# Normalised h made from the transposed chunks instead of turned token rows, indexer keys projected before the norm, query halves doubled by DMA

## Chip, cores and metric

One Trainium2 chip, one core. The number is the device time in microseconds (us) of one execution of the whole kernel.

## What is computed

One layer of a hybrid encoder block on x of 512 tokens by 1024 channels, in fp32. What matters here is the first part, the norm, the input projection and the indexer of the sparse branch:

```python
h = rmsnorm(x, g_pre_mix[l])                  # x * rsqrt(mean(x*x) + eps) * g, one factor per token
proj = h @ w_in[l]
(qa, ka, va, qi, ki, wi, qb, kb, vb, gate_a, gate_b) = split_columns(proj)
# indexer: 8 heads of 64, one shared key of 64, one weight per head and token
dots  = relu(einsum('bqhd,bsd->bqhs', qi, ki) * IDX_DIM ** -0.5)
score = einsum('bqhs,bqh->bqs', dots, wi * N_IDX_HEADS ** -0.5)
top_val, top_idx = lax.top_k(where(admissible, score, -inf), 128)
```

After it come sparse attention over the chosen keys, a stick-breaking attention, gates, an output projection and a SwiGLU MLP of width 2816. The change leaves those alone.

## The kernel before

Every engine (TensorE, ScalarE or ACT, VectorE or DVE, GpSimd or POOL, SyncE or SP) runs a list of instructions written out by hand, and the lists meet at semaphores. Each fp32 product is made of three fp32r products: an operand `a` is split into `a_hi` (rounded by ACT) and `a_lo = a - a_hi` (made by DVE or POOL), and TensorE adds hi*hi, hi*lo and lo*hi. So nothing can be multiplied before ACT has rounded it and DVE or POOL has made the rest.

The start of the kernel goes as follows.

- `first` holds, for each of 8 chunks of 128 channels, the transposed x (512 tokens) beside the indexer-query columns of `w_in` (512 columns). `chunk_rows` (L320) loads a chunk as one 512 KB transfer into a ring `xf` of four. ACT rounds both halves (`round_x` L864 with the gain g folded in, `round_wq` L868), DVE makes `xg_lo` (`rest_x` L1364), POOL makes `wq_lo` (`rest_wq` L1211), and TensorE runs three passes of four 512-column matmuls per chunk (`first_pass` L551, loop L556 to L574) into banks 0 to 3. These queries are not normalised: the token factor r is positive, so it can be moved past the relu into the head weights `w_tok` (L1404).
- The normalised h, for all other projections, is made from token rows: four blocks `x_in` of 128 tokens are loaded, ACT squares them (`square_x` L857), DVE and ACT make r = 1/sqrt(var) per block, DVE scales the rows by r and by the gain (`norm_x` L1368; the gain row was spread over partitions by TensorE, L564 to L568), TensorE turns each block with eight transposes (`turn_x` L537), ACT rounds it (`round_turned` L852) and DVE makes the rest (`rest_turned` L1356). The turns lie between the chunks 2 to 5 of the query projection.
- Then 24 matmuls make the indexer key and head weights from h (L579 to L584, called the kw stage below), and `heads_b_steps` (L603) starts the first two tiles of the other projections, interleaved with `indexer_scores(h)` (L586) for the eight heads. A head's scores are hi and lo query parts against the key; `qi_twice` holds each head's rounded query twice, on partitions 0 to 63 and 64 to 127, and ACT writes both copies out of PSUM (L907 to L910), 16 half-height instructions.
- ACT applies the relu (L923, L924), DVE adds up the weighted scores (L1413 to L1424), 24 instructions, then takes the top 128 in rounds of eight. `indexer_scores(h)` waits for the relu of head h-2.
- The value projection V follows (L633 to L640). Its weight tiles 0 and 1 are rounded by ACT before the queries (L899, L900), tiles 2 and 3 after them and before the first relu (L912, L913). POOL makes the rest of tile 2 only after `idx_summed` reached 8, the end of the score sums (L1251 to L1262).

SP issues the loads in one queue, in order. A weight pair d goes into half of the buffer `raw` and waits for `w_lo_done` of pair d-2 and for the landing of pair d-1 (`pair`, L340 to L350). V's tiles 2 and 3 are the pair of the second turn of the loop at L370.

```python
        for t in range(PAIRS):
            ...
            for h in range(2):
                r, o = slice(HD * h, HD * h + HD), slice(HD - HD * h, P - HD * h)
                run(qi_twice[r, 2 * t + h, :], ps[r, t, :], ACT.Copy).then_inc(qi_hi_done, 1)
                run(qi_twice[o, 2 * t + h, :], ps[r, t, :], ACT.Copy).then_inc(qi_hi_done, 1)
```

Of the kernel before, what the change touches and what calls it, by code (L numbers as in the profile page):

```python
# [28 lines left out]
P = 128  # L29
# [22 lines left out]
WARM = 14  # L52
# [71 lines left out]
def build(nc, first, gain_cols, first_kw, x, w_in, w_branch_sparse, w_branch_sb, w_out, w_gate_up, w_down,  # L124
# [75 lines left out]
    xf = sb("xf", [RING, 1024])  # L200
# [61 lines left out]
    small_in, kw_in, g_cols_in, g_row_in = sems("small_in", "kw_in", "g_cols_in", "g_row_in")  # L262
    first_in = sems(*(f"first_in{c}" for c in range(KC)))
# [55 lines left out]
    def _(sp):  # L319
        def chunk_rows(c):  # L320
# [49 lines left out]
        loop(T_V, KC // 2, v_rows)  # L370
# [75 lines left out]
    def _(pe):  # L446
# [80 lines left out]
        def first_part(k, tile, u, t0, t1):  # L527
# [3 lines left out]
            pe.wait_ge(h_lo_done, k * TB + t1)  # L531
# [46 lines left out]
        pe.wait_ge(h_lo_done, TB)  # L578
        for c in range(KC):  # L579
            acc = ps[0:KW, 6, :]  # L580
            mm(acc, kw_hi[:, c, :], h_hi[:, c, :], start=c == 0, stop=False)
            mm(acc, kw_hi[:, c, :], h_lo[:, c, :], start=False, stop=False)
            ins = mm(acc, kw_lo[:, c, :], h_hi[:, c, :], start=False, stop=c == KC - 1)
        ins.then_inc(kw_done, 1)  # L584

        def indexer_scores(h):  # L586
# [3 lines left out]
            if h == 0:  # L590
                pe.wait_ge(qi_rest_done, 1)
                pe.wait_ge(ki_halves_done, 3)
                pe.wait_ge(w_tok_done, 1)
            if h == 1:
                pe.wait_ge(qi_rest_done, PAIRS)
            for b in (3, 2, 1):
# [163 lines left out]
        for i in range(4):  # L760
            first_part(1, T_UP, i, 0, 2)
# [927 lines left out]
```

## Time and profile before

| | |
|---|---|
| median of three runs | 788.36 us (787.41 to 788.89) |
| the profiled execution, its own time | 788.59 us |
| its span in the trace | 786.8 us |
| TensorE matmul busy | 777.3 us, 99% of the span |
| VectorE, ScalarE, GpSimd busy | 380.5, 357.3, 413.4 us |
| granted TensorE clock, mean | 0.999 |

The span is the time from the first to the last record of the trace; 1.8 us of the execution lie around it. A timeline row gives start and duration in us, the engine, the source line, the operation with output and input names, and in brackets how long the engine had been idle before it and what ended that. Durations of neighbouring matmuls overlap, since they are pipelined; the distance between two starts is what a matmul costs TensorE. A row "x4" merges four in a row.

### The profile page before, as it was taken

To read this page: it belongs to the slowest core of one execution; us is meant where nothing else is said; L and a number is where in the kernel's file an instruction comes from. 1 tells how busy PE (TensorE), PEld (TensorE's weight loads), DVE (VectorE), ACT (ScalarE), POOL (GpSimd) and SP (SyncE) were. 2 spreads that over 40 slices of the span, in tenths; PEclk is the share of its full clock that TensorE was granted. 3 is DMA by queue.
4 is the path that set the end of the run, shared out by engine and by line. 5 is a ranking of instruction groups with operands and counts; after the bars stand their busy time and mean duration, and the time that the engine had idled before them with its cause. 6 is when DMAs were issued, how large, how long until landed. Compare 5 with 4: busy or idle time off the path is not lost.

```text
span 786.8 us, 10511 instructions
## 1 busy us (share of the span) xinstructions
PE 777.3 (99%) x3700; PEld 649.8 (83%) x3700; DVE 380.5 (48%) x540; ACT 357.3 (45%) x572; POOL 413.4 (53%) x250
## 2 busy tenths in 40 slices
PE   9999999999999999999999999999999999999997
PEld 6788888888888888888888988888888888888885
DVE  5689959999566665299137000000000020544564
ACT  6774177767686766542265222222212222232242
POOL 5666255866768687243560334444344443444462
PEclk9999999999999999999999999999999999999999
DMA  9321443113222422212491123333223332233312
GB/s 345 107 100 47 141 121 107 55 54 95 72 62 68 114 61 81 81 54 107 137 318 54 55 66 94 107 107 106 74 86 107 107 107 81 80 107 107 107 54 107
DMA packets 100011, 79.40 MB, mean 101 GB/s; under 512 B 2817, under 2 KB 90889, under 8 KB 99978
## 3 DMA queue, kind: packets, MB, share of 16 engines
q1 hardware_dynamic: 99978, 78.97, 31.9%
q8 instruction: 20, 0.33, 0.2%
q14 instruction: 13, 0.11, 0.0%
HBM read 76.85 MB, written 3.68 MB: 102 GB/s over the span
## 4 chain that ended last, share of the span: by engine, by line
PE 92%; DVE 5%; ACT 1%; issue 0%; DMA 0%; DVEq 0%; SPq 0%
PE ps L478 24%; PE ps L457 19%; PE ps L458 19%; PE ps L459 19%; PE ps L553 2%; PE ps L702 2%; PE ps L691 2%; PE ps L674 1%; PE ps L676 1%; DVE keep_buf L1471 1%; PE ps L498 1%; DVE e_buf L1479 1%; DVE h_lo L1360 1%; PE ps L600 1%; PE ps L599 1%; DVE k_both L1431 0%
## 5 line engine op out<-in xcount | busy, mean ns | idle before, releaser
L1171 POOL TENSOR_TENSOR w_lo<-raw,w_hi 128x1024 fp32r<-128x1024 f32 x74 | 177.1, 2394 | 248.3 <-ACT w_hi L813 219.9
L457 PE MATMUL ps<-h_hi,w_hi 128*128 128x512 f32 (+1 forms) x608 | 235.7, 388 | 0.3 <-DVE h_lo L1360 0.3
L459 PE MATMUL ps<-h_hi,w_lo 128*128 128x512 f32 (+1 forms) x608 | 233.8, 385 | 0.0
L458 PE MATMUL ps<-h_lo,w_hi 128*128 128x512 f32 (+1 forms) x608 | 233.7, 384 | 0.0
L813 ACT ACTIVATE w_hi<-raw 128x1024 fp32r<-128x1024 f32 (+1 forms) x70 | 74.1, 1060 | 271.2 <-PE ps L459 192.1
L459 PEld LDWEIGHTS ps<-h_hi,w_lo 128*128 128x128 f32 x608 | 114.3, 188 | 22.5
L457 PEld LDWEIGHTS ps<-h_hi,w_hi 128*128 128x128 f32 x608 | 114.4, 188 | 21.7 <-issue 0.7
L458 PEld LDWEIGHTS ps<-h_lo,w_hi 128*128 128x128 f32 x608 | 114.4, 188 | 21.0
L1623 DVE TENSOR_TENSOR act<-silu,ps 128x512 f32 (+1 forms) x22 | 15.1, 688 | 211.3 <-PE ps L459 211.3
L1271 POOL TENSOR_TENSOR w_lo<-raw,w_hi 128x1024 fp32r<-128x1024 f32 x30 | 77.7, 2593 | 30.5 <-ACT w_hi L948 30.1
L1628 DVE TENSOR_TENSOR d_lo<-act,d_hi 128x512 fp32r<-128x512 f32 x18 | 43.0, 2395 | 51.7 <-ACT d_hi L1111 51.7
L478 PE MATMUL ps<-w_hi,d_hi 128*128 128x512 f32 x144 | 44.4, 389 | 0.0
L478 PE MATMUL ps<-w_lo,d_hi 128*128 128x512 f32 x144 | 44.4, 389 | 0.0
L478 PE MATMUL ps<-w_hi,d_lo 128*128 128x512 f32 x144 | 44.3, 389 | 0.0
L1180 POOL TENSOR_TENSOR q_lo<-proj,q_twice 64x512 fp32r<-64x512 f32 x16 | 26.8, 1675 | 29.6 <-ACT q_twice L827 28.5
L1508 DVE TENSOR_TENSOR a_lo<-ps,a_hi 128x1280 fp32r<-128x1280 f32 x16 | 23.8, 1489 | 23.7 <-ACT a_hi L995 23.6
L995 ACT ACTIVATE a_hi<-ps 128x1280 fp32r<-128x1280 f32 x16 | 19.9, 1246 | 28.3 <-PE ps L691 28.3
L948 ACT ACTIVATE w_hi<-raw 128x1024 fp32r<-128x1024 f32 x30 | 31.9, 1063 | 0.2
L478 PEld LDWEIGHTS ps<-w_lo,d_hi 128*128 128x128 f32 x144 | 27.0, 188 | 5.7
L478 PEld LDWEIGHTS ps<-w_hi,d_lo 128*128 128x128 f32 x144 | 27.0, 188 | 5.6
L478 PEld LDWEIGHTS ps<-w_hi,d_hi 128*128 128x128 f32 x144 | 27.0, 188 | 5.6
L1471 DVE TENSOR_TENSOR_SCAN keep_buf<-keep_buf,ends 128x1280 f32<-128x1280 f32 x8 | 26.1, 3268 | 10.6 <-ACT keep_buf L976 10.5
(212 smaller groups left out, 1342.9 us busy)
## 6 DMA issues: line engine op xcount, KB each, us to landing
raw<-in_w_gate_up SPq DMA_DIRECT2D x44, 512.0 KB, 4.5
raw<-in_w_in SPq DMA_DIRECT2D x40, 512.0 KB, 4.2
raw<-in_w_down SPq DMA_DIRECT2D x22, 512.0 KB, 3.9
xf<-in_first SPq DMA_DIRECT2D x8, 512.0 KB, 6.1
raw<-in_w_out SPq DMA_DIRECT2D x8, 512.0 KB, 4.1
x_in<-in_x SPq DMA_DIRECT2D x4, 512.0 KB, 7.7
raw<-in_w_branch_sb SPq DMA_DIRECT2D x8, 256.0 KB, 3.0
raw<-in_w_branch_sparse SPq DMA_DIRECT2D x8, 256.0 KB, 2.9
```

Source lines behind the costliest of these rows:

```text
L457: mm(acc, whi_c, a_hi_, start=first, stop=False)
L458: mm(acc, whi_c, a_lo_, start=False, stop=False)
L459: return mm(acc, wlo_c, a_hi_, start=False, stop=last)
L478: ins = mm(bank(2 * t + n), a[:, t * P:(t + 1) * P], w[:, slot, n * 512:(n + 1) * 512], start=first and p == 0, stop=last and p == 2)
L813: run(w_hi[:, at(u), :], raw[:, at((d % 2) * 2 + u), :], ACT.Copy).then_inc(w_hi_done, 1)
L948: run(hi[:, slot, :], raw[:, (T_FILL + k) % 4, :], ACT.Copy).then_inc(w_hi_done, 1)
L1171: nc.gpsimd.tensor_tensor(w_lo[:, at(u), :], raw[:, at((d % 2) * 2 + u), :], w_hi[:, at(u), :], sub).then_inc(w_lo_done, 1)
L1180: nc.gpsimd.tensor_tensor(q_lo[r, h, :], proj[r, 2 * g, :], q_twice[r, h, :], sub).then_inc(q_lo_done, 1)
L1271: nc.gpsimd.tensor_tensor(lo[:, slot, :], raw[:, (T_FILL + k) % 4, :], hi[:, slot, :], sub).then_inc(w_lo_done, 1)
L1471: nc.vector.tensor_tensor_scan(keep_buf[:, ::-1], keep_buf[:, ::-1], ends[:, ::-1], 1.0, ALU.mult, ALU.max).then_inc(scan_done, 1)
L1508: tt(a_lo[:, :], z(1, 0, TRI), a_hi[:, :], sub).then_inc(a_lo_done, 1)
L1628: tt(d_lo[:, at(u), :], act[:, at(j * 2 + u), :], d_hi[:, at(u), :], sub).then_inc(d_lo_done, 1)
```

## The change

- The rows are no longer normalised or turned. When all four blocks are squared, r is made for all tokens at once; DVE lays it as four diagonal matrices (`diag`), and one fp32 matmul of `ones` against them (inside chunk 5) puts r of every token on all partitions in bank 7. Then DVE makes h for a chunk as x_t * g * r into banks 4 and 5 in turn (`make_h`), ACT rounds it (`round_h`) and DVE makes the rest (`rest_h`): a ring of three steps per chunk, eight chunks.
- The gain row and its matmuls are gone. All of transposed x stays in `x_t`; a chunk is loaded as two transfers of 256 KB.
- The kw stage works on xg, the x before the norm; DVE then multiplies the key by r (`ki`), and the head weights take r twice. `kw_lo` moves from DVE to POOL.
- ACT rounds each pair of query heads once, full height, into `qi_hi` (`round_qi`); SP then copies it into `qi_twice` with four transfers of 64 partitions for each pair, 16 in all, from SBUF to SBUF, each of 128 KB. They stand in SP's queue behind V's tiles 0 and 1 and ahead of V's tiles 2 and 3. `qi_lo` has full height, and the zeros are in `ki_hi` now.
- TensorE warms up with nine fp32 matmuls on a tile of zeros, released by DVE, instead of 14 transposes of `ident`, released by POOL. The head weights are turned by transposes instead of fp32 matmuls. `gain_cols` is loaded from ACT's queue.
- POOL makes the bias rows in two parts, the second after V's tiles 0 and 1.

```diff
@@ SP
+        def chunk_in(c):
+            sp.dma_start(x_t[:, c, :], first[c, :, 0:S]).then_inc(x_t_in[c], 16)
             if c >= RING:
-                sp.wait_ge(xg_lo_done, c - RING + 1)
                 sp.wait_ge(wq_lo_done, c - RING + 1)
-            sp.dma_start(xf[:, c % RING, :], first[c, :, :]).then_inc(first_in[c], 16)
+            sp.dma_start(wq_raw[:, c % RING, :], first[c, :, S:2 * S]).then_inc(wq_in[c], 16)
...
-        loop(T_V, KC // 2, v_rows)
+        pair(T_V // 2, 0, v_rows)
+        for t in range(PAIRS):
+            sp.wait_ge(qi_hi_done, t + 1)
+            for h in range(2):
+                for o in range(2):
+                    sp.dma_start(qi_twice[HD * o:HD * o + HD, 2 * t + h, :].bitcast(F32),
+                                 qi_hi[HD * h:HD * h + HD, t, :].bitcast(F32)).then_inc(qi_twice_in[t], 16)
+        with sp.Fori(1, KC // 2) as j:
+            pair(j + T_V // 2, j, v_rows)
@@ TensorE
-        pe.wait_ge(const, 2)
+        pe.wait_ge(warm_done, 1)
         for _ in range(WARM):
-            nc.tensor.transpose(bank(4)[:, 0:P], ident[:, :], ident[:, :])
+            mm(bank(4)[:, 0:P], warm[:, :], warm[:, :], start=True, stop=True)
...
             first_pass(wq_hi, xg_hi, c, c == 0, False)
+            if c == 5:
+                pe.wait_ge(small_kept, 1)
+                pe.wait_ge(diag_done, 1)
+                mm(bank(7), ones[:, :], diag[:, :, :].rearrange("p t n -> p (t n)"), start=True, stop=True).then_inc(r_spread, 1)
...
-            if c == 0:
-                pe.wait_ge(g_row_in, 16)
-                for n in range(2):
-                    ins = mm(bank(6 + n), one_row[:, :], g_in[:, n * 512:(n + 1) * 512], start=True, stop=True)
-                ins.then_inc(gain_spread, 1)
-            if 2 <= c < 2 + TB:
-                turn_x(c - 2)
-            if c == 2 + TB:
+            if c == 1:
+                pe.wait_ge(const, 2)
+                nc.tensor.transpose(bank(5, P), ident[:, :], ident[:, :]).then_inc(ident_turned, 1)
+            if c == 3:
                 pe.wait_ge(small_in, 16)
...
+            if h % 2 == 0:
+                pe.wait_ge(qi_twice_in[h // 2], 64)
@@ ScalarE
-        for c in range(1, KC):
+        for c in range(1, TB + 1):
             round_x(c)
             round_wq(c)
-            if 2 <= c < 2 + TB:
-                root(0, c - 2)
-            if c <= TB:
-                square_x(c - 1)
-            if c >= TB:
-                round_turned(0, c - TB)
+            square_x(c - 1)
+        sc.wait_ge(var_done[0], 1)
+        run(std[:, 0:TB], var[:, 0:TB], ACT.Sqrt).then_inc(root_done[0], 1)
+        for c in range(TB + 1, KC):
+            round_x(c)
+            round_wq(c)
+            round_h(c - TB - 1)
         sc.wait_ge(kw_in, 16)
         run(kw_hi[:, :, :], kw_raw[:, :, :], ACT.Copy).then_inc(kw_hi_done, 1)
         split(T_QKB // 2, 0)
+        round_h(3)
+        sc.wait_ge(kw_lo_done, 1)
         split(T_QKB // 2, 1)
+        round_h(4)
+        round_qi(0)
...
@@ VectorE
+        def make_h(c):
+            if c >= 2:
+                ve.wait_ge(xh_lo_done, c - 1)
+            stt(bank(4 + c % 2), x_t[:, c, :], g_cols[:, c:c + 1], bank(7), ALU.mult, ALU.mult).then_inc(xh_made, 1)
...
+        for c in range(TB):
             rest_x(c)
...
+        rest_x(TB + 1)
+        ve.wait_ge(r_spread, 1)
+        make_h(0)
+        rest_x(TB + 2)
+        make_h(1)
+        rest_x(TB + 3)
+        for c in range(KC):
+            rest_h(c)
+            if c + 2 < KC:
+                make_h(c + 2)
+            if c == KC - 3:
+                rest_qi(0)
+        ve.wait_ge(kw_done, 1)
+        ve.wait_ge(r_kept, 1)
+        ki = ps[0:HD, 6, :]
+        tt(ki, ki, r_row[0:HD, :], ALU.mult).then_inc(ki_scaled, 1)
```

How the order moves on two queues. First SP, behind the loads of the start: before, from the load of the kw weights on (`ISA` and branch rows are the loop over V's tiles).

```order
L338 DMA kw_raw<-in_first_kw 128x576
L350 DMA raw<-in_w_in 128x8x128 x2
L358 UNCONDITIONAL_BRANCH
L358 ISA
L345 ISA [waits w_lo_done]
L350 ISA [waits raw_in]
L350 ISA
L350 DMA raw<-in_w_in 128x2x512
```

The same place now.

```order
L349 DMA kw_raw<-in_first_kw 128x576
L361 DMA raw<-in_w_in 128x8x128 x2
L361 DMA raw<-in_w_in 128x2x512 [waits raw_in]
L361 DMA raw<-in_w_in 128x2x512
L386 DMA qi_twice<-qi_hi 64x512 [waits qi_hi_done]
L386 DMA qi_twice<-qi_hi 64x512 x3
...
L386 DMA qi_twice<-qi_hi 64x512 [waits qi_hi_done]
L386 DMA qi_twice<-qi_hi 64x512 x3
L388 UNCONDITIONAL_BRANCH
```

Sixteen copies, in four groups that each wait for ACT, stand ahead of the loop that now loads V's tiles from tile 2 on.

Second ACT, from the last chunk's rounding to the first relu, before (the rows L909 and L910 are the 16 half-height query copies, eight of each, the other six pairs left out).

```order
L866 ACTIVATE xg_hi<-xf,g_cols 128x512
L869 ACTIVATE wq_hi<-xf 128x512
L855 ACTIVATE h_hi<-ps 128x8x128
L885 ACTIVATE kw_hi<-kw_raw 128x576
L813 ACTIVATE w_hi<-raw 128x1024 x2
L895 ACTIVATE wv_hi<-raw 128x1024 x2
L909 ACTIVATE qi_twice<-ps 64x512
L910 ACTIVATE qi_twice<-ps 64x512
...
L895 ACTIVATE wv_hi<-raw 128x1024 x2
L923 ACTIVATE relu_buf<-ps 128x896
```

The same place now (L880 and L884 round a chunk, L888 is `round_h`, L892 `round_qi`).

```order
L880 ACTIVATE xg_hi<-x_t,g_cols 128x512
L884 ACTIVATE wq_hi<-wq_raw 128x512
L888 ACTIVATE h_hi<-ps 128x512
L910 ACTIVATE kw_hi<-kw_raw 128x576
L827 ACTIVATE w_hi<-raw 128x1024
L888 ACTIVATE h_hi<-ps 128x512
L827 ACTIVATE w_hi<-raw 128x1024
...
L931 ACTIVATE wv_hi<-raw 128x1024 x2
L936 ACTIVATE wi_t<-ps 8x512
L931 ACTIVATE wv_hi<-raw 128x1024 x2
L948 ACTIVATE relu_buf<-ps 128x896
```

The rounding of h now stands, chunk by chunk, between the rounding of the inputs and ahead of the kw weights; V's tiles 2 and 3 still stand directly ahead of the first relu.

## Rows read from the trace of the kernel before

**Rows 1.** The page, part 1; and TensorE's waits from 60 us on.
```profile
PE 777.3 (99%) x3700; PEld 649.8 (83%) x3700; DVE 380.5 (48%) x540; ACT 357.3 (45%) x572; POOL 413.4 (53%) x250
...
PE ps L691 <- DVE att_out L1516: 0.6, 1, 0.6
```

**Rows 2.** Timeline of TensorE, 0 to 12 us (start, duration, engine, line, operation).
```profile
1.68 3.25 PE L549 MATMUL ps<-ident 128*128 128x128 f32 x14 [1.68 <-POOL ident L1166]
5.08 2.07 PE L553 MATMUL ps<-xg_hi,wq_hi 128*128 128x512 f32 x4 [0.16 <-ACT xg_hi L866]
...
9.20 1.98 PE L567 MATMUL ps<-g_in,one_row 1*128 1x512 f32 x4
11.10 1.19 PE L553 MATMUL ps<-xg_hi,wq_hi 128*128 128x512 f32 x4
```

**Rows 3.** Timeline of TensorE, 13 to 35 us.
```profile
13.94 1.07 PE L553 MATMUL ps<-xg_hi,wq_hi 128*128 128x512 f32 x4
...
16.67 1.03 PE L543 MATMUL ps<-ident,x_in 128*128 128x128 f32 x8
17.46 1.17 PE L553 MATMUL ps<-xg_hi,wq_hi 128*128 128x512 f32 x4
...
24.46 1.06 PE L543 MATMUL ps<-ident,x_in 128*128 128x128 f32 x8 [0.40 <-DVE h_lo L1360]
...
34.86 0.40 PE L581 MATMUL ps<-h_hi,kw_hi 128*72 128x512 f32 x1
```

**Rows 4.** Timeline of TensorE, 40 to 73 us.
```profile
40.43 0.40 PE L457 MATMUL ps<-h_hi,w_hi 128*128 128x512 f32 x1
...
43.26 1.05 PE L618 MATMUL ps<-ident,wi_t 8*128 8x8 f32 x8
...
47.09 0.39 PE L599 MATMUL ps<-ki_both,qi_twice 128*128 128x512 f32 x1
...
51.27 0.39 PE L599 MATMUL ps<-ki_both,qi_twice 128*128 128x512 f32 x1
...
72.06 0.70 PE L478 MATMUL ps<-wv_hi,h_hi 128*128 128x512 f32 x2
```

**Rows 5.** Timeline of ScalarE, 22 to 51 us.
```profile
22.28 0.71 ACT L866 ACTIVATE xg_hi<-xf,g_cols 128x512 fp32r<-128x512 f32 x1
...
46.05 2.00 ACT L895 ACTIVATE wv_hi<-raw 128x1024 fp32r<-128x1024 f32 x2
48.33 0.92 ACT L923 ACTIVATE relu_buf<-ps 128x896 f32<-128x896 f32 x1 [0.28 <-PE ps L600]
49.15 0.38 ACT L924 ACTIVATE relu_buf<-ps 128x256 f32<-128x256 f32 x1
...
50.47 0.63 ACT L818 ACTIVATE proj<-ps 128x512 f32<-128x512 f32 x1
```

**Rows 6.** Timeline of VectorE, 15 to 66 us.
```profile
15.41 0.75 DVE L1366 SCALAR_TENSOR_TENSOR xg_lo<-xf,g_cols,xg_hi 128x512 fp32r<-128x512 f32 x1 [0.29 <-ACT xg_hi L866]
...
37.53 1.39 DVE L1410 TENSOR_TENSOR qi_lo<-ps,qi_twice 64x512 fp32r<-64x512 f32 x2 [5.00 <-ACT qi_twice L910]
...
52.77 12.44 DVE L1423 SCALAR_TENSOR_TENSOR score<-relu_buf,w_tok,score 128x512 f32<-128x512 f32 x21
```

**Rows 7.** Timeline of GpSimd, 27 to 75 us.
```profile
27.80 1.28 POOL L1213 TENSOR_TENSOR wq_lo<-xf,wq_hi 128x512 fp32r<-128x512 f32 x1 [2.94 <-ACT wq_hi L869]
...
69.52 4.76 POOL L1235 TENSOR_TENSOR wv_lo<-raw,wv_hi 128x1024 fp32r<-128x1024 f32 x2
```

**Rows 8.** SP's queue, 2 to 4 and 36 to 45 us (start, duration, line).
```profile
3.34 0.42 SPq L325 DMA_DIRECT2D xf<-in_first  x1
...
37.20 1.08 SPq L350 DMA_DIRECT2D raw<-in_w_in  x2
```

**Rows 9.** Stretches of 0.5 us; last three numbers: granted clock, DMA share, GB/s.
```profile
39.00:39.50 0.50, 0.50 (x3) 0.28 (x2) 0.00 (x0) 0.47 (x2) 0.50 (x2) 1.00 0.91 352
...
41.50:42.00 0.50, 0.50 (x4) 0.42 (x3) 0.50 (x1) 0.48 (x2) 0.50 (x3) 1.00 0.07 21
```

More of the change, by code:

```diff
@@ L51 @@
 KW = HD + HEADS
-WARM = 14
+WARM = 9
 RING = 4
@@ L185, in build @@
     wi_t = sb("wi_t", S)
+    r_row = sb("r_row", S)
     top[0] = zone2 + 4 * 2 * TRI
@@ L577, in _ @@
         pe.wait_ge(kw_lo_done, 1)
-        pe.wait_ge(h_lo_done, TB)
         for c in range(KC):
             acc = ps[0:KW, 6, :]
-            mm(acc, kw_hi[:, c, :], h_hi[:, c, :], start=c == 0, stop=False)
-            mm(acc, kw_hi[:, c, :], h_lo[:, c, :], start=False, stop=False)
-            ins = mm(acc, kw_lo[:, c, :], h_hi[:, c, :], start=False, stop=c == KC - 1)
+            mm(acc, kw_hi[:, c, :], xg_hi[:, c, :], start=c == 0, stop=False)
+            mm(acc, kw_hi[:, c, :], xg_lo[:, c, :], start=False, stop=False)
+            ins = mm(acc, kw_lo[:, c, :], xg_hi[:, c, :], start=False, stop=c == KC - 1)
         ins.then_inc(kw_done, 1)
@@ L615, in _ @@
         pe.wait_ge(wi_t_done, 1)
-        pe.wait_ge(small_kept, 1)
+        pe.wait_ge(xh_made, KC)
+        pe.wait_ge(r_kept, 1)
         for t in range(TB):
-            ins = mm(ps[:, 7, t * HEADS:(t + 1) * HEADS], wi_t[HD:KW, t * P:(t + 1) * P],
-                     ident[HD:KW, HD:KW], start=True, stop=True)
+            ins = nc.tensor.transpose(ps[:, 7, t * HEADS:(t + 1) * HEADS], wi_t[HD:KW, t * P:(t + 1) * P],
+                                      ident[HD:KW, HD:KW])
         ins.then_inc(wi_done, 1)
@@ L864, in round_x, with round_h, round_qi @@
         def round_x(c):
-            sc.wait_ge(first_in[c], 16)
-            run(xg_hi[:, c, :], xf[:, c % RING, 0:S], ACT.Copy, scale=g_cols[:, c:c + 1]).then_inc(xg_hi_done, 1)
+            sc.wait_ge(x_t_in[c], 16)
+            run(xg_hi[:, c, :], x_t[:, c, :], ACT.Copy, scale=g_cols[:, c:c + 1]).then_inc(xg_hi_done, 1)
         def round_wq(c):
-            run(wq_hi[:, c, :], xf[:, c % RING, S:2 * S], ACT.Copy).then_inc(wq_hi_done, 1)
+            sc.wait_ge(wq_in[c], 16)
+            run(wq_hi[:, c, :], wq_raw[:, c % RING, :], ACT.Copy).then_inc(wq_hi_done, 1)
+        def round_h(c):
+            sc.wait_ge(xh_made, c + 1)
+            run(h_hi[:, c, :], bank(4 + c % 2), ACT.Copy).then_inc(xh_hi_done, 1)
+        def round_qi(t):
+            sc.wait_ge(chunk_done, KC)
+            run(qi_hi[:, t, :], bank(t), ACT.Copy).then_inc(qi_hi_done, 1)
+        sc.dma_start(g_cols[:, :], gain_cols).then_inc(g_cols_in, 16)
         nc.scalar.preload_act_table(ACT.Sqrt)
@@ L886, in _ @@
         split(T_QKB // 2, 0)
+        round_h(3)
+        sc.wait_ge(kw_lo_done, 1)
         split(T_QKB // 2, 1)
+        round_h(4)
+        round_qi(0)
+        round_h(5)
+        round_qi(1)
+        round_h(6)
+        round_qi(2)
+        round_h(7)
+        run(r_row[0:HD, :], ps[0:HD, 7, :], ACT.Copy).then_inc(r_kept, 1)
+        round_qi(3)
         def split_value(c):
@@ new lines, in _ @@
+        nc.vector.tensor_copy(ki_hi[0:HD, 0, :], ki).then_inc(ki_hi_done, 1)
+        nc.vector.tensor_copy(ki_both[0:HD, :], ki).then_inc(ki_halves_done, 1)
+        nc.vector.tensor_copy(ki_hi[HD:P, 1, :], ki).then_inc(ki_halves_done, 1)
+        ve.wait_ge(ki_hi_done, 1)
+        tt(ki_both[HD:P, :], ki, ki_hi[0:HD, 0, :], sub).then_inc(ki_halves_done, 1)
+        for t in range(1, PAIRS):
+            rest_qi(t)
+        ve.wait_ge(wi_done, 1)
+        for b in range(TB):
+            r = rstd[:, b:b + 1]
+            ins = ts(w_tok[:, b, :], ps[:, 7, b * HEADS:(b + 1) * HEADS], r, r, ALU.mult, ALU.mult)
@@ L1615, in _ @@
         second_norm(3)
[L1616 to L1617 removed]
+        rest_turned(2)
+        rest_turned(3)
         def up(j):
```

211 lines of the change are left out of this document (97 added, 114 removed).

## The prediction

> **What bounds the kernel.** I read the page first, then TensorE's waits, then the timelines of the first 75 us. TensorE is busy 99% of the span, and from 60 us on its largest wait is 0.6 us [rows 1]. So only two things can change the time: what TensorE issues less, and new idle time of TensorE. Both lie in the first 72 us; whatever the start of V's tile 2 (72.06, [rows 4]) gains or loses, the rest of the kernel carries along unchanged. A measurement here can tell 0.2%, 1.6 us, from no change. The sum is made against the profiled execution (788.59 us, 0.23 above the median).
>
> **To the start of chunk 1.** Before, 14 transposes took 3.25 us from 1.68 on, the first pass began at 5.08, and chunk 0 took until 9.20: 4.12 us for twelve matmuls that cost 2.73 at full speed (13.94 to 16.67, [rows 3]); the difference is the 1.2 GHz level [rows 2]. Two gain matmuls followed until 11.10, four records in 1.90 us, so an fp32 matmul is two records and costs 0.95 [rows 2]. Now the warm-up needs no `ident` and starts near 0.95. Nine fp32 matmuls are 18 records at 3.25/14 = 0.23: they end near 5.0, and the first pass starts about where it did. Chunk 0 costs between 2.73 (clock up before it) and 4.12; I take 3.4, the middle, since the activity starts 0.7 us earlier. The gain matmuls are gone. Chunk 1 starts at 8.4 instead of 11.10, bounds 7.8 and 9.1: **2.7 us earlier**. ACT can follow: it has no work between its chunks but the squares.
>
> **From chunk 1 to the kw stage.** Before it took 23.76 us (11.10 to 34.86): seven chunks of 2.73 are 19.1; four turns of 0.79 (16.67 to 17.46) are 3.2; a wait of 0.40; the small matmul and slower restarts are the other 1.1 [rows 2, 3]. The change removes turns, wait and restarts and adds one fp32 matmul (0.95) and one transpose (0.1): 20.5 without waits. But three waits are new.
> - DVE may not go past `small_turned` after chunk 3, and everything for r (rest of chunk 4, five small DVE and ACT steps, the diagonals) stands behind it: ACT, blocked on `var_done`, rounds chunk 5 some 2.9 us after chunk 3 ended. TensorE loses about 0.2.
> - r is spread inside chunk 5. Then `make_h(0)` (DVE, 0.76 like [rows 6], 15.41), `round_h(0)` (ACT, 0.63 like the 512-column copy from PSUM), `xg_hi` (0.71, [rows 5]) and `wq_hi` (0.6) run one behind the other, 2.8 us with their handshakes, while TensorE has 1.8 us left in chunk 5: 1.0 lost. In chunk 6 the same ring takes 2.8 and TensorE 2.75: nothing lost.
> - `kw_hi` stands behind `round_h(2)`, which waits for `make_h(2)` and `rest_h(0)`, and `kw_lo` is now POOL's: 576 columns at 1.28 for 512 [rows 7] are 1.44, before 0.75 on DVE. `kw_lo` ends at 31.7, TensorE is there at 30.0: 1.7 lost.
> Together 23.4, and the kw stage starts at 31.8 instead of 34.86: **3.1 earlier**. Most of what the turns gave goes into waits of the ring. If a DVE step with PSUM on both sides costs 1.0 instead of 0.76, another 0.7 to 1.5 is lost.
>
> **From the kw stage to the first scores.** kw costs 5.57 as before (34.86 to 40.43). The first four steps run against `h_lo`, which stays ahead. Then TensorE waits 0.5 for `wi_t` (ACT makes it behind four h chunks, four query copies, `r_row` and V's tiles 0 and 1), and four transposes save about 0.5 of eight fp32 records (1.05, [rows 4]). ACT's 16 half copies (0.6 each, 9.9 us with kw's) become four of 0.63. On DVE the key scaling adds 0.7, the query rests fall from eight of 0.70 [rows 6] to four; `w_tok` is ready at 43.9. First scores at 44.0 instead of 47.09: still **3.1 earlier**.
>
> **The SP queue and the first relu.** This step decides. ACT's first relu waits for V's tiles 2 and 3 being rounded (2.00 us, [rows 5]), and they for their load. Before, the load was issued at 37.20 and had landed at 41.55, 1 MB in 2.6 us [rows 8, 9], 4.5 us before ACT wanted it (46.05). Now 16 copies of 128 KB stand ahead of it. The first pair is rounded at 33.85; issuing costs 0.42 each [rows 8], data flow begins 1.7 us after an issue (37.20, and full flow by 39.0). The trace has no transfer from SBUF to SBUF and none of 64 partitions, so I bound a copy from the loads, 1.28 us for 512 KB over 128 partitions, 4 KB in each:
> - by bytes, a quarter: 0.32, hidden below the issue of 0.42;
> - by bytes in a partition, half: 0.64.
> I take 0.64, because a copy touches half the partitions at both its ends, so half the lanes idle twice. Then 16 copies end at 35.6 + 10.2 = 45.8, the load at 48.4 to 48.6, the roundings at 50.5, and the first relu starts at 50.5 instead of 48.33. The scores of head 2 wait for its end (1.2 later, [rows 5]): they start at 51.7 instead of 51.27 [rows 4], and TensorE, which could have started at 48.1, idles 3.6. DVE's sums (12.44 for seven heads, [rows 6]) follow in the same rhythm; the first one, slower before beside POOL, is no longer the limit. V's tile 2 still waits for POOL's 6.7 us behind the sums, and both arrive at 72.5. All 3.1 us are given back and 0.4 more: 788.6 + 0.4 = 789.0, or 788.9 against the median. **Forecast: no change.**
>
> The Trainium skill ("SBUF — State Buffer", Door 1: The DMA port swizzle) says that partitions 0 to 63 reach only 8 of 16 ports and measured 196 GB/s for them against 328 for all 128, at 1 MiB. At 196 GB/s a copy would take 0.67, an estimate from that page, and the sum would be 0.5 us more; by bytes alone it would be the first rival's time. No run here shows such a transfer yet.
>
> **Other edits.** Splitting a chunk into two loads adds eight issues of 0.42 in SP's queue, hidden: the queue is ahead of the data until chunk 4, and TensorE needs chunk 7 only at 27. Loading the gains from ACT brings them earlier, below the warm-up. POOL's bias rows end at 52 instead of 46 and are wanted by SP only at 76. Memsets moved in POOL lie in its idle time.
>
> **Rivals.**
> - *A: the copies go by bytes (0.32) or at least as fast as they are issued.* Then the load lands near 45.0, the first relu starts at 47.0, TensorE waits 0.2 or not at all and keeps 3.1 us: 785.5. For it: every load seen reaches 400 GB/s, and nothing is read from HBM. Against it: nothing in the trace fills only half the partitions. Anything between 0.42 and 0.64 gives 785.5 to 789.
> - *B: the copies cost more than 0.72 each.* A round trip per copy that isn't hidden would do it. Each 0.1 more delays the load, the first relu and V by 1.6 us; from 0.72 on the kernel is slower by over 0.2%; at 0.8 it is 788.6 + 0.4 + 2.6 = 791.6.
> - *C: TensorE's idle time of 3.6 us before head 2 drops its clock to 1.2 GHz.* No wait in this trace is that long. The price is that of chunk 0, 4.12 - 2.73 = 1.4, or more: 790.4.
>
> **How the numbers follow.** Forecast 0.50 (0.06 of it below 786.8, 0.38 within 0.2%, 0.06 above 789.9: an earlier or later rise of the clock moves it by 0.6, a dearer h ring by up to 0.7). A 0.33, of which 0.31 is faster. B 0.11 and C 0.06 are slower. Sums: faster 0.37, same 0.40, slower 0.23. The forecast's own range is 787.9 to 790.2. For 8 in 10 the range takes in A down to 784.9 and the lower part of B up to 791.2.
>
> **What would show it.** Right: chunk 1 at about 8.4, kw at about 31.8, the transfer records of the copies running back to back for some 10 us from 35.6, the loads of tiles 2 and 3 landing after 48, a wait of 3 to 4 us of TensorE at head 2's scores released by ACT's relu, and V's tile 2 near 72.5. Wrong: the copies done by 43, or that wait missing (A); the wait over 5 us (B); 512-column matmuls 0.43 apart after it (C); kw later than 33, which would put the error into the h ring.

## Result and profile after

The changed kernel takes **792.67 us** (median; 792.07 to 793.47) against 788.36 in the same session (787.41 to 789.88): ratio 1.0055, 95% interval 1.004 to 1.007. It is 4.3 us slower. The forecast was 788.9 with no change as the likeliest verdict, and 784.9 to 791.2 as its range; the time lies outside of it.

The page's first part answers to [rows 1]:

```profile
span 790.8 us, 10447 instructions
...
PE 775.8 (98%) x3667; PEld 648.0 (82%) x3667; DVE 374.1 (47%) x540; ACT 350.4 (44%) x562; POOL 412.2 (52%) x251
```

So do TensorE's waits (us in total, times, longest):

```profile
PE ps L610 <- ACT relu_buf L949: 4.1, 1, 4.1
PE ps L589 <- POOL kw_lo L1254: 1.3, 1, 1.3
PE ps L558 <- DVE warm L1397: 1.1, 1, 1.1
PE ps L562 <- ACT wq_hi L884: 0.9, 1, 0.9
PE ps L542 <- DVE y_buf L1388: 0.6, 1, 0.6
PE ps L610 <- DVE w_tok L1462: 0.5, 1, 0.5
```

TensorE is busy 1.5 us less than before (775.8 for 777.3), and yet the span is 4.0 longer: one wait of 4.1 us, before the scores of head 2, stands out. TensorE's timeline shows where the 3.1 us that the prediction gave to the first scores went (it answers to [rows 2, 3, 4]):

```profile
1.07 4.21 PE L558 MATMUL ps<-warm 128*128 128x128 f32 x18 [1.07 <-DVE warm L1397]
4.93 2.05 PE L562 MATMUL ps<-xg_hi,wq_hi 128*128 128x512 f32 x4
6.78 1.20 PE L562 MATMUL ps<-xg_lo,wq_hi 128*128 128x512 f32 x4
7.82 1.07 PE L562 MATMUL ps<-xg_hi,wq_lo 128*128 128x512 f32 x4
...
25.43 0.93 PE L562 MATMUL ps<-xg_hi,wq_hi 128*128 128x512 f32 x3 [0.86 <-ACT wq_hi L884]
...
32.48 0.42 PE L589 MATMUL ps<-xg_hi,kw_hi 128*72 128x512 f32 x1 [1.27 <-POOL kw_lo L1254]
...
44.80 0.47 PE L610 MATMUL ps<-ki_both,qi_twice 128*128 128x512 f32 x1 [0.48 <-DVE w_tok L1462]
...
53.34 0.80 PE L610 MATMUL ps<-ki_both,qi_twice 128*128 128x512 f32 x1 [4.12 <-ACT relu_buf L949]
53.94 0.63 PE L611 MATMUL ps<-ki_hi,qi_lo 128*128 128x512 f32 x1
...
57.35 0.63 PE L476 MATMUL ps<-h_hi,w_hi 128*128 128x512 f32 x1
...
59.81 0.39 PE L610 MATMUL ps<-ki_both,qi_twice 128*128 128x512 f32 x1
```

| | before | predicted | after |
|---|---|---|---|
| chunk 1 | 11.10 | 8.4 | 8.72 |
| kw stage | 34.86 | 31.8 | 32.48 |
| first scores | 47.09 | 44.0 | 44.80 |
| first relu (ACT) | 48.33 | 50.5 | 52.09 |
| scores of head 2 | 51.27 | 51.7 | 53.34 |
| V's tile 2 | 72.06 | 72.5 | 76.33 |

Up to the first scores the kernel is 2.3 us ahead. At head 2 it is 2.1 behind, and 2.2 more are lost behind that: the 512-column matmul there takes 0.63 where it takes 0.39 at 59.81, so heads 2 and 3 need 4.01 us (53.34 to 57.35). The other end of the wait is SP's queue and ACT; these rows of their timelines answer to [rows 8, 5]:

```profile
34.42 10.15 SPq L386 DMA_DIRECT2D qi_twice<-qi_hi  x16
45.21 6.24 SPq L361 DMA_DIRECT2D raw<-in_w_in  x4
...
50.07 2.00 ACT L931 ACTIVATE wv_hi<-raw 128x1024 fp32r<-128x1024 f32 x2 [9.16 <-DMA raw<-in_w_in]
52.09 0.92 ACT L948 ACTIVATE relu_buf<-ps 128x896 f32<-128x896 f32 x1
```

SP issues 16 copies in 10.15 us, and only then the loads of V's tiles 2 and 3, at 45.21. The issues themselves, summed up over the line:

```profile
L386 SPq DMA_DIRECT2D qi_twice<-qi_hi x16: 539/597/605, 34.4 to 44.0; - x16
...
DMA to landing us min/median/max: 2.2/2.3/2.4
```

Every copy lands 2.2 to 2.4 us after its issue, the last like the first. So no queue of transfers builds up in front of the DMA engines: SP is the one that is held, 0.60 us in each issue, 0.635 from one to the next. By windows of 1 us (after the window come its length, the busy time of TensorE, weight loads, DVE, ACT and POOL with the number of instructions, the granted clock, DMA share and GB/s), it looks like this, where [rows 9] had 352 GB/s in a load:

```profile
38.00:39.00 1.00, 1.00 (x6) 0.81 (x5) 1.00 (x2) 1.00 (x2) 1.00 (x4) 1.00 0.87 205
42.00:43.00 1.00, 1.00 (x6) 0.81 (x5) 1.00 (x2) 0.00 (x0) 1.00 (x2) 1.00 0.89 209
...
46.00:47.00 1.00, 1.00 (x8) 0.91 (x8) 0.00 (x0) 0.00 (x0) 1.00 (x5) 1.00 0.65 72
47.00:48.00 1.00, 1.00 (x7) 0.82 (x6) 0.00 (x0) 0.00 (x0) 1.00 (x5) 1.00 0.96 358
...
51.00:52.00 1.00, 0.00 (x0) 0.00 (x0) 0.00 (x0) 1.00 (x2) 1.00 (x4) 0.71 0.60 72
...
52.00:53.00 1.00, 0.00 (x0) 0.00 (x0) 0.00 (x0) 0.97 (x3) 1.00 (x5) 0.50 0.85 324
...
55.00:56.00 1.00, 1.00 (x5) 0.90 (x5) 1.00 (x3) 0.33 (x1) 0.00 (x0) 0.50 0.08 18
...
58.00:59.00 1.00, 1.00 (x5) 0.78 (x5) 0.75 (x3) 0.78 (x2) 0.00 (x0) 0.88 0.00 0
```

Two things are in it. The copies run at 205 GB/s, as the forecast had it, and between them and the load the flow falls to 72 GB/s (46 to 47). And the granted clock falls to 0.50, the 1.2 GHz level, while TensorE has been idle since 49.2, and comes back at 58 to 59.

### The profile page after: what moved, and what is told of

Read it like the earlier page. It is cut to its first block, busy times and chain, and to the rows that moved or that the text cites. A ratio compares the mean times of both kernels' runs of the same rounds, so it can differ in the third digit from the quotient of the medians.

```text
span 790.8 us, 10447 instructions
## 1 busy us (share of the span) xinstructions
PE 775.8 (98%) x3667; PEld 648.0 (82%) x3667; DVE 374.1 (47%) x540; ACT 350.4 (44%) x562; POOL 412.2 (52%) x251
## 4 chain that ended last, share of the span: by engine, by line
PE 90%; DVE 5%; ACT 2%; SPq 1%; issue 1%; DMA 1%; POOL 0%; DVEq 0%
PE ps L497 23%; PE ps L476 18%; PE ps L478 18%; PE ps L477 18%; PE ps L716 2%; PE ps L705 2%; PE ps L562 2%; SPq L386 1%; PE ps L688 1%; PE ps L690 1%; DVE keep_buf L1523 1%; PE ps L517 1%; DVE e_buf L1531 1%; PE ps L610 1%; PE ps L558 1%
## 5 line engine op out<-in xcount | busy, mean ns | idle before, releaser
L1680 DVE TENSOR_TENSOR d_lo<-act,d_hi 128x512 fp32r<-128x512 f32 x18 | 43.1, 2396 | 51.7 <-ACT d_hi L1136 51.7
```

Source lines behind the costliest of these rows:

```text
L1680: tt(d_lo[:, at(u), :], act[:, at(j * 2 + u), :], d_hi[:, at(u), :], sub).then_inc(d_lo_done, 1)
```

## Experiments

Two theories of the loss stood at first. **Issue order** (Q in the expectations): the loads of tiles 2 and 3 stand behind 16 copies, their lateness makes TensorE idle, and the idle time drops the clock. **Rest of the change** (W): the h ring, the key scaling or DVE's longer list lose the time, and the copies only show it. Within the first, it was open what a copy's 0.635 us are made of. Edits are against the changed kernel, and ratios against the kernel before, where nothing else is said.

### e1_order: the loads issued behind the first four copies

```diff
                     sp.dma_start(qi_twice[...], qi_hi[...]).then_inc(qi_twice_in[t], 16)
+            if t == 0:
+                pair(T_V // 2 + 1, 1, v_rows)
-        with sp.Fori(1, KC // 2) as j:
+        with sp.Fori(2, KC // 2) as j:
```

> Only the order in SP's queue changes: the load of V's tiles 2 and 3 is issued after the first four copies instead of after all sixteen. Theory Q (the loads queued behind the copies make the first relu late, and that wait makes the 1.2 GHz stretch): tiles 2 and 3 land near 42, the first relu starts near 46 to 47, TensorE's wait before head 2 is under 1 us, no 1.2 GHz stretch, and the kernel takes 3 us less than the one before, about 785.5. Rival W (the new waits in the first 45 us cost more than they seem, or something after 72 us is slower): at most half of the 4.3 us comes back, 790 or more.

Measured: 785.2 us (784.98 to 786.58), ratio 0.9965 (0.9953 to 0.9976). Nothing is computed differently; only a pair of loads is 12 places further ahead.

SP's and ACT's timelines:

```profile
33.26 2.46 SPq L386 DMA_DIRECT2D qi_twice<-qi_hi  x4
36.06 0.93 SPq L361 DMA_DIRECT2D raw<-in_w_in  x2
37.03 8.04 SPq L386 DMA_DIRECT2D qi_twice<-qi_hi  x12
...
41.82 2.01 ACT L933 ACTIVATE wv_hi<-raw 128x1024 fp32r<-128x1024 f32 x2 [2.08 <-DMA raw<-in_w_in]
44.94 0.92 ACT L950 ACTIVATE relu_buf<-ps 128x896 f32<-128x896 f32 x1 [1.11 <-PE ps L613]
```

ACT's first relu now waits for TensorE's scores (1.11) and starts 7.2 us earlier. The order of one queue costs 7.5 us: 792.67 - 785.2. One more reading is needed further down: the two loads, in the middle of the copies, took only 0.39 and 0.50 us to issue (36.06 to 36.99), where a copy takes 0.60.

### e2_no_copies: no copies at all

SP's loop of copies is gone as well, and with it TensorE's wait for them.

```diff
-                mm(dst, qi_twice[:, h, rows], ki_both[:, 0:n], start=True, stop=False)
+                mm(dst, qi_hi[:, h // 2, rows], ki_both[:, 0:n], start=True, stop=False)
```

> The sixteen copies are left out; TensorE reads the full-height rounded pair instead, so the doubling is left out of what is computed and every other instruction stays. Theory Q: as with the order changed, 785 to 786. If it is clearly faster than the kernel with the order changed, the copies cost something beside the place in the queue. Rival W: 790 or more.

Measured: 785.3 us (784.85 to 785.87), ratio 0.9964 (0.9952 to 0.9976). It is the same time as with the copies behind the loads. So in the right order the 16 copies cost nothing that can be measured, and the rest of the change is worth 3 us.

### e3_fill_wait: the idle time filled with matmuls of no effect

```diff
+            if h == 2:
+                for _ in range(17):
+                    mm(bank(1), qi_hi[HD:P, 0, 0:P], ki_hi[HD:P, 0, :], start=False, stop=False)
             if h >= 2:
                 pe.wait_ge(idx_relu, h - 1)
```

> The changed kernel with 17 matmuls by zeros added in TensorE's idle time before head 2 (3.9 of its 4.1 us), which add nothing to the sums. If the 1.2 GHz stretch comes from the idle time, it goes: heads 2 and 3 take 2.1 us instead of 4.0, and the kernel takes 2.0 to 2.3 us less than the changed one, about 790.4. If the late relu alone makes the loss (DVE's sums, not TensorE, end the stage), it stays near 792.7.

Measured: 789.93 us (789.28 to 790.51), ratio 1.0019 (1.001 to 1.0029).

TensorE's timeline (L598 are the fillers):

```profile
48.27 4.14 PE L598 MATMUL ps<-ki_hi,qi_hi 64*128 64x512 f32 x17
52.66 0.50 PE L613 MATMUL ps<-ki_both,qi_twice 128*128 128x512 f32 x1 [0.24 <-ACT relu_buf L952]
53.00 0.40 PE L614 MATMUL ps<-ki_hi,qi_lo 128*128 128x512 f32 x1
...
56.96 0.39 PE L613 MATMUL ps<-ki_both,qi_twice 128*128 128x512 f32 x1
```

TensorE still cannot go on before 52.66, but its clock stays up (0.40 for the 512-column matmul), and 2.7 us are gone between the medians: 792.67 - 789.93. In the two profiled executions, 2.96 us apart, 0.7 of it is not the clock: this run was ahead from chunk 1 on (8.04 for 8.72), and head 2 started at 52.66 instead of 53.34. From there to head 4 it takes 4.30 us (52.66 to 56.96) instead of 6.47 (53.34 to 59.81), 2.2 less. That is the price of the lower clock in this pair. The trace of the changed kernel gives as much without an experiment: 4.01 - 2.10 for the two heads and 2.46 - 2.08 for the three steps behind them, 2.3 us.

### e4_full_height: 8 copies of 128 partitions

The bytes are the same; left out is the doubling, since the halves are not swapped. TensorE waits for two copies of a pair instead of four.

```diff
-                for o in range(2):
-                    sp.dma_start(qi_twice[HD * o:HD * o + HD, 2 * t + h, :], qi_hi[HD * h:HD * h + HD, t, :])
+                sp.dma_start(qi_twice[:, 2 * t + h, :], qi_hi[:, t, :])
```

> The same bytes copied from SBUF to SBUF in 8 transfers of 128 partitions instead of 16 of 64 (each half then holds another head, so the doubling is left out of what is computed). Theory H (a transfer's time goes by the partitions that it covers at either end): about 400 GB/s, all done in some 5.5 us, the loads of tiles 2 and 3 issued near 40, the first relu near 47, time near 785.5. Rival S (a transfer from SBUF to SBUF runs at 205 GB/s whatever its height): GB/s stays at 205, 10 us in all, time as the changed kernel, 792.7.

Measured: 785.35 us (785.03 to 787.0), ratio 0.9966 (0.9955 to 0.9977).

The issues, and a window of 1 us among them:

```profile
L385 SPq DMA_DIRECT2D qi_twice<-qi_hi x8: 465/608/615, 34.9 to 39.4; - x8
```

```profile
38.00:39.00 1.00, 1.00 (x6) 0.76 (x5) 1.00 (x3) 1.00 (x3) 1.00 (x4) 1.00 1.05 404
```

Twice the rate, 404 GB/s. It looks like a proof that half the partitions give half the rate. It isn't one: an issue takes 0.61 us here too, and each carries twice the bytes. The landings stay at 2.3 to 2.4 us after the issue, so 404 GB/s is what the issues bring, and not yet a limit of the height. The next runs take the two apart.

### e5_half_width: half the bytes, still 64 partitions

Here and in e12b_from_hbm TensorE reads the undoubled `qi_hi`, as in e2_no_copies.

```diff
-                    sp.dma_start(qi_twice[..., 2 * t + h, :], qi_hi[..., t, :])
+                    sp.dma_start(qi_twice[..., 2 * t + h, 0:S // 2], qi_hi[..., t, 0:S // 2])
```

> The change with its 16 copies cut to half of their columns, so half of the bytes over the same 64 partitions (left out: the second halves of the copies, and TensorE reads the undoubled query tiles instead). The full copies were spaced 0.635 us and moved 205 GB/s. Theory M (what moves the bytes through 64 partitions sets the 0.635, and SP is held by it): a copy takes about 0.42, the issue cost of any load, the 16 take some 7 us instead of 10.2, the loads of tiles 2 and 3 are issued near 41, the first relu near 48.6 and the time is about 789. Theory I (0.635 is a fixed cost of issuing such a copy): the spacing stays 0.63, everything stays where it was, 792.5.

Measured: 791.31 us (790.69 to 791.76), ratio 1.0033 (1.0019 to 1.0047).

SP's timeline, and the same window:

```profile
33.83 10.12 SPq L386 DMA_DIRECT2D qi_twice<-qi_hi  x16
```

```profile
38.00:39.00 1.00, 1.00 (x6) 0.84 (x5) 0.97 (x2) 1.00 (x2) 1.00 (x4) 1.00 0.36 92
```

Half the bytes, and the 16 issues take 10.12 instead of 10.15 us, with the DMA engines busy 0.36. Theory M, on which my 0.64 rested, falls: the spacing is a cost of issuing. Theory I expected 792.5 and got 791.3: the first copy went out at 33.83 instead of 34.42 in this run, behind a chunk 1 that was 0.7 earlier (8.06). The rest is the clock: from head 2 to head 4 TensorE took 5.71 us (52.77 to 58.48) instead of 6.47, so the 1.2 GHz level cost less in this execution.

### e13_all_partitions and e12b_from_hbm: is it the height or the source?

```diff
-                    sp.dma_start(qi_twice[HD * o:HD * o + HD, 2 * t + h, :], qi_hi[HD * h:HD * h + HD, t, :])
+                    sp.dma_start(qi_twice[:, 2 * t + h, o * 256:o * 256 + 256], qi_hi[:, t, o * 256:o * 256 + 256])
```

> The change with 16 copies of the same 128 KB, but laid over all 128 partitions with half of the columns each (left out: the doubling; the copied tiles hold the halves unswapped). Theory F (the spacing of 0.635 us is a fixed cost of an issue at this place, whatever the bytes, the height or the source): still 0.635 each, the loads of tiles 2 and 3 behind them, the DMA engines idle for half of the time (share below 0.6 instead of 0.88), and the time about 791.3 to 792.5. Theory H (64 partitions make the issue dear, and the full-height copies of e4_full_height were held at 0.64 by their 256 KB at 400 GB/s): the spacing falls to 0.47, the loads are issued 2.6 us earlier and the time is 789 to 790.

Measured: 792.46 us (790.59 to 793.51), ratio 1.0045 (1.0026 to 1.0065); the copies are again 0.636 apart (10.18 us for 16). The DMA engines' share by windows was 0.47 to 0.71, so below 0.6, as expected, only in part of them.

```diff
-                                 qi_hi[HD * h:HD * h + HD, t, :])
+                                 first[t, HD * h:HD * h + HD, 0:S])
```

> The change with its 16 copies reading the same 128 KB each from HBM (rows of the first input chunks) instead of from qi_hi (left out: the doubling; TensorE reads the undoubled query tiles). The half-width copies kept the spacing of 0.635 us at half of the bytes, so the spacing is a cost of the issue. Theory S (it belongs to copies whose source is in SBUF): the spacing falls to 0.47, as for the loads at the start, the loads of tiles 2 and 3 are issued 2.6 us earlier and the time is 789.5 to 790.5. Theory P (it belongs to transfers onto 64 partitions, or to this place of the program): the spacing stays at 0.63 and the time at 792.5.

Measured: 792.53 us (791.56 to 792.82), ratio 1.0055 (1.004 to 1.0071).

SP's timeline in e13_all_partitions, then the issues of e12b_from_hbm:

```profile
34.84 10.18 SPq L386 DMA_DIRECT2D qi_twice<-qi_hi  x16
```

```profile
L386 SPq DMA_DIRECT2D qi_twice<-in_first x16: 552/596/606, 33.9 to 43.5; - x16
```

Changing the height alone or the source alone doesn't shorten the issue: 0.60 us and 0.635 to 0.65 apart in all five forms (64 partitions from SBUF with 64 or 128 KB, 64 partitions from HBM, 128 partitions from SBUF with 128 or 256 KB). That leaves two readings. One is theory P's "this place of the program" and theory F of e13. Against it stand the two loads of e1_order, which took 0.39 and 0.50 at this very place. They come from HBM and cover 128 partitions, as do the loads at the start with 0.42 to 0.43 in most cases. So the other reading fits every one of these rows: a source in SBUF, or a height of 64, is each enough for 0.60. No run changed both at once in the copies, and it stays open.

### e11b_two_pairs: the same copies in 8 issues of 256 KB

TensorE looks for the copies at every fourth head instead of every second.

```diff
-        for t in range(PAIRS):
-            sp.wait_ge(qi_hi_done, t + 1)
+        for t in range(0, PAIRS, 2):
+            sp.wait_ge(qi_hi_done, t + 2)
...
-                    sp.dma_start(qi_twice[..., 2 * t + h, :], qi_hi[..., t, :])
+                    sp.dma_start(qi_twice[..., 2 * t + h:2 * t + h + 3:2, :], qi_hi[..., t:t + 2, :])
```

> The change with 8 copies instead of 16, each of 64 partitions and two query tiles (256 KB). Bytes and result are as in the change, the number of issues is half. If issuing at 0.635 us were all that costs, 8 issues end 5 us earlier and the loads land near 45: the first relu starts at 47 to 48 and the time is 786. If 64 partitions also move only about 230 GB/s (the 16 copies kept the DMA engines busy to 0.88 at 205 GB/s, and the half-width ones to 0.4 at 103), the 2 MB take 9 us whoever issues them, the loads land near 47.5 to 48.5 behind them, and the time is 788.5 to 790.5.

Measured: 791.14 us (790.76 to 792.39), ratio 1.004 (1.0025 to 1.0055).

The issues with their landings, then two windows:

```profile
L386 SPq DMA_DIRECT2D qi_twice<-qi_hi x8: 596/856/1237, 35.0 to 41.3; - x8
...
DMA to landing us min/median/max: 3.1/4.7/5.1
```

```profile
38.00:39.00 1.00, 1.00 (x6) 0.84 (x5) 0.96 (x3) 1.00 (x3) 1.00 (x5) 1.00 0.97 190
42.00:43.00 1.00, 1.00 (x6) 0.83 (x5) 1.00 (x3) 0.00 (x0) 1.00 (x2) 1.00 0.97 238
```

Here the limit of 64 partitions shows: landings grow from 3.1 to 5.1 us after the issue, the engines are busy 0.97 at 190 to 238 GB/s. The last landing is at 41.3 + 5.1 = 46.4, so 2.1 MB take some 9.7 us from the first data (35.0 + 1.7): about 216 GB/s, an estimate. And now the bytes do show in the issue: SP is held 0.60 to 1.24 us in each, though e4_full_height issued the same 256 KB over 128 partitions in 0.61. Halving the issues saved 1.5 us of 7.4. The two ceilings lie side by side: 205 GB/s by the issue, about 216 by the height. The time is above the 788.5 to 790.5 expected: the first relu started at 51.39, the first copy having waited for the second query pair.

The Trainium skill ("SBUF — State Buffer", Door 1: The DMA port swizzle) has 196 GB/s for partitions 0 to 63 against 328 for all 128, at 1 MiB, a ratio of 0.60. Here it is 216 to 404, 0.53, and the 404 may not be a ceiling yet. The trace agrees that 64 partitions bound the rate, once enough bytes stand behind an issue, and by somewhat more than those two figures say.

### e6_load_by_act: the loads issued by another queue

```diff
-        with sp.Fori(1, KC // 2) as j:
+        with sp.Fori(2, KC // 2) as j:
...
+        for u in range(2):
+            sc.dma_start(raw[...], rows[...]).then_inc(raw_in, 16)
         split_value(2)
```

> The change with its 16 copies as they are, but the loads of V's tiles 2 and 3 issued from ACT's queue behind wi_t (about 41), as early as my prediction had SP issue them. Theory H (what I had wrong is only that SP is held at every copy, so that the load waits for all 16 to be issued): the load shares the engines with the copies, lands by 46 to 47, the first relu starts near 49 and the time is 787 to 789.5. Theory Q (the transfers themselves stand in the way, whoever issues): the load lands no earlier than 49, the first relu starts after 51 and the time is 791.5 to 793.

Measured: 785.74 us (784.78 to 786.25), ratio 0.9966 (0.9953 to 0.9978).

SP's and ACT's timelines:

```profile
33.32 10.41 SPq L386 DMA_DIRECT2D qi_twice<-qi_hi  x16
...
37.23 0.98 ACTq L942 DMA_DIRECT2D raw<-in_w_in  x2
...
44.46 2.01 ACT L931 ACTIVATE wv_hi<-raw 128x1024 fp32r<-128x1024 f32 x2 [4.65 <-DMA raw<-in_w_in]
46.49 0.92 ACT L956 ACTIVATE relu_buf<-ps 128x896 f32<-128x896 f32 x1
```

All 16 copies stay, and the loads pass them. They were issued at 37.23, 4 us earlier than I meant: ACT's own queue runs ahead of its compute, and the wait for `w_lo_done` was already met. That is why the time is below the 787 to 789.5 expected. Between 39 and 43 the two streams together moved 252 to 379 GB/s, more than the copies alone, so the copies left room. The copies themselves landed later, up to 6.9 us after their issue (median 4.9) instead of 2.3, but no engine waited for one.

### e9_old_warm_up, e8_kw_early, e10b_tokens_first: the other terms of the sum

These three start from e1_order. e9 puts back the 14 transposes of `ident`. e8 rounds `kw_hi` ahead of h chunk 2. e10b is e8 with `w_tok` ahead of the last two query rests on DVE.

```diff
 # e8, ACT
             round_wq(c)
+            if c == KC - 1:
+                sc.wait_ge(kw_in, 16)
+                run(kw_hi[:, :, :], kw_raw[:, :, :], ACT.Copy).then_inc(kw_hi_done, 1)
             round_h(c - TB - 1)
-        sc.wait_ge(kw_in, 16)
-        run(kw_hi[:, :, :], kw_raw[:, :, :], ACT.Copy).then_inc(kw_hi_done, 1)
```

> e1_order with the warm-up of before: 14 transposes of ident, released by POOL at 1.7. Theory W (the new warm-up lets the first pass begin no earlier but leaves the clock higher through chunk 0: 3.79 us instead of 4.12, 0.5 us to the start of chunk 1): chunk 1 starts near 9.2 and the time is 785.7. Rival (what is lost at the start is caught up, because the squares, r and the h ring set the kw stage, or DVE the first scores): chunk 1 at 9.2, but first scores at 43.6 as in e1_order and 785.2.

> e1_order (785.2) with kw_hi rounded ahead of the h chunk 2 on ACT, so that kw_lo on POOL begins about 1.4 us earlier and TensorE's wait of 1.3 before the kw stage goes. Theory K (that wait is time lost, as my sum had it): kw starts 1.3 earlier and so does everything behind it, 783.9. Theory V (DVE works without a gap from 27.0 to 43.4 on the h chunks, the keys, the query rests and w_tok, and w_tok releases the first scores): kw starts 1.3 earlier, TensorE then waits about 1.8 instead of 0.5 for w_tok, and the time stays at 785.0 to 785.3.

> e8_kw_early (785.2, first scores at 43.1 behind w_tok) with w_tok made on DVE ahead of the last two query rests instead of behind them. If DVE's queue sets the first scores, they start near 42.0, the scores of head 1 wait for the rests until about 43.4, and the time falls by up to 0.5, to 784.7. If the sums of the eight heads behind ACT's relus, or POOL behind them, set the start of V's tile 2, nothing changes: 785.2.

Measured: e9 785.92 us, ratio 0.9966 (0.9954 to 0.9979); e8 785.18, ratio 0.9959 (0.9944 to 0.9974); e10b 784.98, ratio 0.9958 (0.9944 to 0.9971); e1 had 0.9965.

For e9 the intervals decide nothing. Chunk 1 begins at 8.68 there, not at 9.2, and between 7.6 and 9.0 in the twelve profiles with the new warm-up, whose instructions up to there are the same. In four of the twelve (e4, e10b, e11b, e13) 0.3 to 0.6 of it is a wait for ACT's `wq_hi`. The start isn't the same twice, and a gain of 0.5 us from the warm-up alone can't be read from that. Inconclusive.

In e8 the wait for `kw_lo` is gone and kw starts at 29.67 instead of 31.31. DVE's timeline shows why the first scores gain only 0.5 (43.09 for 43.61), 0.3 of it from chunk 1, which was that much earlier in this run:

```profile
26.70 0.68 DVE L1414 TENSOR_TENSOR h_lo<-ps,h_hi 128x512 fp32r<-128x512 f32 x1
27.42 0.76 DVE L1410 SCALAR_TENSOR_TENSOR ps<-x_t,g_cols,ps 128x512 f32<-128x512 f32 x1
...
40.14 1.89 DVE L1418 TENSOR_TENSOR qi_lo<-ps,qi_hi 128x512 fp32r<-128x512 f32 x3
41.94 0.86 DVE L1465 TENSOR_SCALAR w_tok<-ps,rstd 128x8 f32<-128x8 f32 x4
```

From 26.70 to 42.8 DVE has no gap: h chunks, keys, query rests, `w_tok`. Its list, not the kw stage, releases the first scores, and the time is the one of theory V. The wait isn't: instead of 1.8 us for `w_tok`, TensorE waits 0.55 for a query rest at 35.94, 0.30 for `wi_t` and 0.48 for `w_tok`. In e10b `w_tok` is no wait any more, and the time stays. Its first scores did not come near 42.0 but at 44.00: chunk 1 was 1.2 later than in e8, the waits of 0.53 and 0.32 further ahead remained, and from chunk 1 on only 0.3 was gained. That the time stays fits the other expectation (the sums of the eight heads, or POOL behind them), which no run tested by itself. The three are equal within their intervals, and about 0.4% faster than the kernel before; e1_order is the shortest edit that gets nearly all of it.

## Why the prediction was wrong

Two terms failed, and they add up to the miss. The load behind the copies was put 1.6 us too early, because SP was thought to run ahead at 0.42 us an issue. And the sum put the lower clock at nothing, where it cost 2.2 to 2.3. With the first alone the time would have been 790.6, inside the range; with the clock held up, e3 is at 789.93, inside it too.

**Chunk 1 (8.4) and the ring (kw at 31.8): right.** 8.72 lies in the bounds of 7.8 to 9.1, and the waits at chunk 6 (predicted 1.0, measured 0.86) and at kw (1.7; 1.27) are where they were put, released by the instructions that were named. kw is 0.7 late, 0.3 of it from chunk 1. Hitting chunk 1 to 0.3 is partly luck, with starts from 7.6 to 9.0 in the twelve profiles. The idea that what `kw_lo` costs is lost for good was wrong, though harmless: in e8 the wait went and the time stayed. Against the median the sum gives 788.8, not 788.9; nothing hangs on it.

**A copy at 0.64 us, "because a copy touches half the partitions": right number by luck, wrong step.** The 0.635 is SP's time for the issue of such a copy. It is shown by e5, e13 and e12b, which halve the bytes, double the height, or change the source, and keep it. I had bounded the issue by the 0.42 of [rows 8] and looked for the rest in the transfer. The limit of 64 partitions is real, and 128 KB at e11b's 216 GB/s would take 0.61, so the two costs happen to lie side by side. Rival A fell by the issue alone, since it needed copies as fast as 0.42; rival B, over 0.72 a copy, fell by the same 0.635.

**"Copies end at 45.8, the load at 48.4 to 48.6": the first step that failed, 1.6 us.** I had SP run ahead at 0.42 an issue, with the loads issued near 41 and lying ready in the queue, so that their first data follows on the last copy. With 0.635 SP is held, the loads are issued at 45.21, and their own 1.7 us to the first data, which the forecast had hidden, lies open: full flow comes after 47 and ACT can round at 50.07. First copy 0.5 us later than assumed and 1.1 us of unhidden latency make the 1.6 at the first relu (52.09 for 50.5). e6 confirms it: with the same 16 copies and the loads issued in time, the loss is gone.

**The clock: the second step that failed, and the dearer one, 2.3 us.** The forecast itself had TensorE idle 3.6 us, and rival C said that this drops the clock, at 0.06. It was taken for another case, and it was a consequence of the same wait. The clock fell in each of the five profiles with such a wait. What it cost is the longer way from head 2 to head 4:

| | wait before head 2 | head 2 to head 4 |
|---|---|---|
| e3_fill_wait (filled, clock 1.00) | 0.24 | 4.30 |
| the changed kernel | 4.12 | 6.47 |
| e5_half_width | 4.19 | 5.71 |
| e11b_two_pairs | 3.84 | 5.82 |
| e12b_from_hbm | 4.45 | 5.63 |
| e13_all_partitions | 4.26 | 5.83 |

So the price was 2.2 us in one execution and 1.3 to 1.5 in four, which is what rival C took from chunk 0 (1.4 or more). Whether 3.6 us would have dropped the clock too, no run shows; 3.84 did. Sum: 788.6 + 0.4 as forecast, 1.6 for the later relu, 2.3 for the slow heads by the trace: 792.9 against the 792.67 of the profiled execution.

**Other edits: right.** The split loads, gains from ACT's queue, POOL's bias rows and moved memsets appear in no wait of TensorE; e2, which keeps them all, is 3 us faster than before.

## What to carry to other kernels

Small DMAs ahead of a big one in an issuing engine's queue cost that engine's time per issue, here 0.6 us each even at half the bytes; what is needed first goes ahead of them, or through another engine's queue. From the landing after each issue one reads which it is: in these runs constant landings (2.2 to 2.4 us) went with a held issuer, growing ones (3.1 to 5.1) with held transfers. And where a forecast has TensorE idle for several microseconds, price the slower clock behind it as part of the forecast, not as another case.

## What the runs showed of the hardware

- The issue of a copy on SP took 0.60 us, 0.635 with its gap, one behind the other at 34 to 45 us: over 64 partitions with 64 or 128 KB from SBUF or 128 KB from HBM, over 128 with 128 or 256 KB from SBUF. Loads from HBM over 128 partitions took 0.39 and 0.50 in the same stretch (e1), and 0.42 to 0.43 for most in the first 4 us. With 256 KB over 64 partitions, where the transfers backed up, an issue took 0.60 to 1.24 (e11b).
- Copies inside SBUF reached 404 GB/s over 128 partitions (e4) and about 216 over 64 (e11b, an estimate).
- After 3.8 to 4.5 us without a matmul the granted clock was 0.50 in five profiles, and the way from head 2 to head 4 took 1.3 to 2.2 us more than the 4.30 at full clock.
- With the same instructions up to there, chunk 1 began anywhere from 7.6 to 9.0 us in twelve profiles.
